# Six seams of a two-block network on one core: the last expert by columns and pieces, halves turned one by one, the last output tile in two parts

## The reference

```
for layer in (0, 1):                      # first block
    mix = windowed_gqa_sink(x) if layer == 0 else bidir_rglru_block(x)
    x = layer_norm(ALPHA * x + mix)
    aff = softmax(x @ w_router)           # 16 experts
    gates, idx = top_k(aff.T, 32)         # each expert picks 32 of the 256 tokens
    g, u = split(x[idx] @ w_gate_up)      # 16 x (1024 x 2048)
    out = (silu(g) * u) @ w_down * gates  # 16 x (1024 x 1024)
    x = layer_norm(ALPHA * x + scatter_add(out, idx))
for layer in (0, 1):                      # second block: even, then odd
    shift, scale, gate = split(silu(c) @ ada_w + ada_b)
    h = layer_norm_2(x) * (1 + scale) + shift
    y = even_mixer(h, ...) if layer == 0 else odd_mixer(h, ...)
    x = layer_norm_2(ALPHA * x + gate * y) * post_ln_g + post_ln_b
```

## Time and profile before

| what | value |
| --- | --- |
| median of 3 runs | 1498.08 us (1497.95 to 1499.9) |
| profiled execution | 1502.24 us, its span 1500.9 us |
| TensorE busy | 1139.1 us, 76% of the span |
| VectorE busy | 461.7 us, 31% |
| ScalarE busy | 326.6 us, 22% |
| granted TensorE clock, mean | 0.89 of 2.4 GHz |
| read from memory | 498.92 MB, 333 GB/s over the span |
| share of the chain of waits | DMA 50%, PE 39%, DVE 7%, ACT 3% |

### The profile page before, as it was taken

One profiled execution on the slowest core, in us unless ns is written; L12 is line 12 of the kernel. 1 busy time (PEld: TensorE's weight loads), 2 busy tenths in 40 slices (PEclk: granted clock), 3 DMA queues, 4 the chain that ended last, 5 costly groups with the idle time before them and its releaser, 6 DMA issues.

```text
span 1500.9 us, 19478 instructions
## 1 busy us (share of the span) xinstructions
PE 1139.1 (76%) x8579; PEld 651.7 (43%) x8579; DVE 461.7 (31%) x919; ACT 326.6 (22%) x627; POOL 65.5 (4%) x88
## 2 busy tenths in 40 slices
PE   8998856678585556999885655665565699989997
PEld 7756311244132111798551112111111289745896
DVE  4535202101120100587530100100000067564674
ACT  4421110001310000365110000000000046443450
POOL 3000100000000000022000000000000000000000
PEclk9999978789787979899998878888888899999999
DMA  9957999999999999929999999999999954214630
GB/s 300 358 198 280 388 425 424 427 417 422 426 422 427 425 425 424 318 59 334 412 410 425 427 424 428 427 425 426 427 427 425 410 196 148 78 50 145 214 109 29
DMA packets 89197, 501.29 MB, mean 334 GB/s; under 512 B 6950, under 2 KB 15604, under 8 KB 56344
## 3 DMA queue, kind: packets, MB, share of 16 engines
q1 hardware_dynamic: 84320, 492.78, 81.2%
q10 hardware_dynamic: 3112, 5.96, 1.1%
q0 software_dynamic: 1680, 1.30, 0.3%
HBM read 498.92 MB, written 1.10 MB: 333 GB/s over the span
## 4 chain that ended last, share of the span: by engine, by line
DMA 50%; PE 39%; DVE 7%; ACT 3%; issue 1%; POOL 1%; SPq 0%; DVEq 0%; ACTq 0%
DMA weight_spare<-in_moe_w_gate_up 16%; DMA weight_ring<-in_moe_w_gate_up 13%; DMA weight_spare<-in_moe_w_down 10%; DMA weight_ring<-in_moe_w_down 6%; PE bank L335 5%; PE bank L1340 5%; PE bank L611 3%; PE bank L336 3%; PE bank L338 3%; PE bank L337 3%; PE bank L1366 3%; DMA weight_ring<-in_even_w_in 2%; PE bank L1746 2%; PE bank L381 2%; DMA weight_spare<-in_ada_w 1%; DVE weight_ring_rounded L376 1%
## 5 line engine op out<-in xcount | busy, mean ns | idle before, releaser
L1340 PE MATMUL bank<-weight_ring,expert_tokens 128*32 128x512 f32 x1904 | 286.3, 736 | 172.8 <-DMA weight_ring<-in_moe_w_gate_up 167.8
L1340 PEld LDWEIGHTS bank<-weight_ring,expert_tokens 128*32 128x32 f32 x1904 | 61.6, 123 | 372.8 <-DMA weight_ring<-in_moe_w_gate_up 205.1
L1366 PE MATMUL bank<-weight_ring,actT 128*32 128x256 f32 x1920 | 155.1, 482 | 69.4 <-DMA weight_ring<-in_moe_w_down 60.6
L1530 DVE TENSOR_TENSOR act<-silu,bank 128x256 f32<-128x256 f32 x32 | 13.4, 420 | 414.9 <-ACT silu L1655 414.9
L1366 PEld LDWEIGHTS bank<-weight_ring,actT 128*32 128x32 f32 x1920 | 72.8, 133 | 139.6 <-issue 54.8
L1655 ACT ACTIVATE silu<-bank 128x256 f32<-128x256 f32 x32 | 12.3, 384 | 463.4 <-PE bank L1340 463.4
L1541 DVE COPY expert_outs<-bank 32x256 f32<-32x256 f32 x64 | 26.8, 418 | 255.8 <-PE bank L1366 254.7
L376 DVE TENSOR_TENSOR weight_ring_rounded<-weight_ring,weight_ring_rounded 128x1024 fp32r<-128x1024 f32 (+1 forms) x76 | 88.2, 1222 | 17.1 <-ACT weight_ring_rounded L360 16.9
L360 ACT CAST weight_ring_rounded<-weight_ring 128x1024 fp32r<-128x1024 f32 (+1 forms) x72 | 69.9, 1044 | 24.6 <-DMA weight_ring<-in_attn_w_qkv 12.0
L1669 ACT COPY expert_outs<-bank 32x256 f32<-32x256 f32 x64 | 23.3, 363 | 233.2 <-PE bank L1366 232.4
L381 PE MATMUL bank<-ident 128*128 128x128 f32 x434 | 56.0, 290 | 3.9 <-DMA ident<-in_k_ident 3.9
(11 more groups left out here) (519 smaller groups left out, 1834.4 us busy)
## 6 DMA issues: line engine op xcount, KB each, us to landing
weight_ring<-in_moe_w_gate_up SPq DMA_DIRECT2D x119, 2048.0 KB, 32.4
weight_ring<-in_moe_w_down SPq DMA_DIRECT2D x60, 2048.0 KB, 32.1
weight_spare<-in_moe_w_gate_up SPq DMA_DIRECT2D x9, 2048.0 KB, 35.6
weight_ring<-in_ada_w SPq DMA_DIRECT2D x8, 2048.0 KB, 13.2
weight_ring<-in_even_w_in SPq DMA_DIRECT2D x5, 2048.0 KB, 14.1
weight_ring<-in_odd_w_in SPq DMA_DIRECT2D x5, 2048.0 KB, 8.5
weight_spare<-in_ada_w SPq DMA_DIRECT2D x4, 2048.0 KB, 17.4
weight_ring<-in_lru_w_in SPq DMA_DIRECT2D x4, 2048.0 KB, 24.5
```

The costliest lines, as they stand in the source:

```text
L1340: last = pe.matmul(up[CAP * j:CAP * (j + 1), :], B.xs[:, t, e * CAP:(e + 1) * CAP], w[:, t % 2, :, j, :], start=(t == 0), stop=(t == T - 1))
L1366: last = pe.matmul(K[3][CAP * q:CAP * (q + 1), 0:QC], B.actT[i][:, s, j * CAP:(j + 1) * CAP], w[:, jj, s, q, :], start=(j == 0 and s == 0) ...
```

## The change

1. The `down` units of expert 15, in both layers, hold one half of the columns each (512) with all rows, and SyncE loads each in four transfers, one for each `j`. TensorE takes the pieces as they land, in products of 128 columns (`last_outs_tensor`), columns 0 into bank 3 and columns 1 into bank 1. The products with `back` for columns 0 stand after the first piece of columns 1. Copies and moments go by column halves, the moments of both halves of the tokens on VectorE in both layers.
2. `turn_x_tensor` and `modulated_tensor` turn half 0 when it is ready, with a number of identity products between the halves. The other identity products are fewer: 26 to 14 and 36 to 34 after the expert layers, 12 to 2 before the recurrent products, 12 to none and 16 to 3 around the even stage's turns, 36 to 24 and 16 to 3 around the odd stage's, 14 to 8 in layer 0's routing; between the halves stand 8, 3 and 16.
3. `x_low` is formed in four quarters: the first before the logits, the three others between the two parts of `hot`. The gather waits for each quarter where it needs it.
4. In `FIRST_UNITS` of layer 1 two `ada` units stand ahead of two expert units.
5. ScalarE rounds a pair of modulated tiles as soon as it is there.
6. In the odd stage half 1's second column half is computed, gated, added and measured in two parts of 256 columns, the last normalising step and the store go by column halves, and statistics are of 256 columns each.

```diff
-    ((2, 0), (None, 6), (3, 2), (4, SPARE), (None, 3), (5, 0), (None, 1), (None, 4), (None, 5), (0, 2), (1, SPARE),
+    ((2, 0), (None, 6), (3, 2), (4, SPARE), (None, 3), (5, 0), (None, 1), (0, 2), (1, SPARE), (None, 4), (None, 5),
...
-    def turn_x_tensor(self, stage, banks):
+    def turn_x_tensor(self, stage, banks, between=0):
 
         sig, pe, x = self.sig, self.pe, self.B.x
         for half in range(H):
+            if half:
+                self.idle_products_tensor(banks[5], between)
...
+            if name.startswith("down") and name.split("_")[1] == str(NE - 1):
+                (dst, src), = self.unit_parts(name, B.slot[slot])
+                for i in range(PACK):
+                    sp.dma_start(dst[:, i], src[:, i]).then_inc(*sig.tell(f"last{name[-1]}{i}_loaded", ("arrived", name, i), by=16))
+                continue
...
+        sp.wait_ge(*sig.after("x", "odd", 0))
+        sp.dma_start(out[:, 0, :], B.x[:, 0, :]).then_inc(*sig.tell("output_stored", ("stored",), by=16))
+        for c in range(2):
+            cols = slice(c * 512, (c + 1) * 512)
+            sp.wait_ge(*sig.after("last_tokens", c))
+            sp.dma_start(out[:, 1, cols], B.x[:, 1, cols]).then_inc(*sig.tell("output_stored", ("stored",), by=16))
...
+            if e == NE - 1:
+                rows = d["moe_w_down"][layer][e].rearrange("(j c s) n -> c j s n", j=PACK, s=2)
+                return [(slot.rearrange("p (j s n) -> p j s n", j=PACK, s=2), rows[:, :, :, k * 512:(k + 1) * 512])]
...
-            self.idle_products_tensor(K[5], 14)
+            self.idle_products_tensor(K[5], 8)
...
-        pe.wait_ge(*sig.after("x_low", stage, 1))
...
+            if e == NE - 1:
+                self.last_outs_tensor(layer)
+                next(side, None)
+                break
...
-        self.idle_products_tensor(K[5], 36 if layer else 26)
+        self.idle_products_tensor(K[5], 34 if layer else 14)
+    LAST_BANKS = (3, 1)
+    def last_outs_tensor(self, layer):
+        sig, pe, B, K = self.sig, self.pe, self.B, self.B.bank
+        stage, e, grp = f"moe{layer}", NE - 1, (NE - 1) // PACK
+        def pieces(c, js):
+            name = f"down{layer}_{e}_{c}"
+            w = self.plain(name).rearrange("p (j s q n) -> p j s q n", j=PACK, s=2, q=PACK)
+            for j in js:
+                pe.wait_ge(*sig.after("arrived", name, j))
+                for s in range(2):
+                    for q in range(PACK):
+                        last = pe.matmul(K[self.LAST_BANKS[c]][CAP * q:CAP * (q + 1), 0:P], B.actT[e % 2][:, s, j * CAP:(j + 1) * CAP],
+                                         w[:, j, s, q, :], start=(j == 0 and s == 0), stop=(j == PACK - 1 and s == 1))
+            if j == PACK - 1:
+                last.then_inc(*sig.tell("experts_down", ("last_down", stage, c), ("free", name)))
+        def back(c):
+            for q in range(2):
+                pe.wait_ge(*sig.after("last_outs", stage, c, q))
+            for half in range(H):
+                pe.matmul(K[self.SUM_BANKS[2 * half + c]], B.back[:, grp, half * P:(half + 1) * P],
+                          B.outs[grp % 2][:, c * 512:(c + 1) * 512], start=False, stop=True).then_inc(
+                    *sig.tell("experts_back", ("summed", stage, half, c)))
+        pe.wait_ge(*sig.after("back", stage, 1))
+        for before in range(1, PACK):
+            for q in range(2):
+                pe.wait_ge(*sig.after("outs", stage, e - before, q))
+        self.idle_products_tensor(K[5], 2)
+        pieces(0, range(PACK))
+        pieces(1, (0,))
+        back(0)
+        pieces(1, range(1, PACK))
+        self.idle_products_tensor(K[5], 2)
+        back(1)
+    def last_outs(self, c, q):
+        r, o = (NE - 1) % PACK, c * 512 + q * P
+        return (self.B.outs[(NE - 1) // PACK % 2][CAP * r:CAP * (r + 1), o:o + P],
+                self.B.bank[self.LAST_BANKS[c]][CAP * q:CAP * (q + 1), 0:P])
...
+                    pe.wait_ge(*sig.after("x_low", stage, half, 2 * t // T))
...
-        def low(half):
+        def low(half, part):
+            tiles = slice(part * T // 2, (part + 1) * T // 2)
             v.wait_ge(*sig.after("x_high", stage, half))
-            v.tensor_tensor(B.x_low[:, half], B.x[:, half, :].rearrange("p (c t) -> p t c", t=T), B.x_high[:, half], ALU.subtract).then_inc(
-                *sig.tell("x_low", ("x_low", stage, half)))
+            v.tensor_tensor(B.x_low[:, half, tiles], B.x[:, half, :].rearrange("p (c t) -> p t c", t=T)[:, tiles],
+                            B.x_high[:, half, tiles], ALU.subtract).then_inc(*sig.tell("x_low", ("x_low", stage, half, part)))
 
...
+        v.wait_ge(*sig.after("router_parts", stage, 0))
+        low(0, 0)
-        low(0)
...
-        low(1)
...
+            if part == 0:
+                for half, tiles in ((0, 1), (1, 0), (1, 1)):
+                    low(half, tiles)
...
+        def outs(c):
+            v.wait_ge(*sig.after("last_down", stage, c))
+            for q in (0, 2):
+                v.tensor_copy(*self.last_outs(c, q)).then_inc(*sig.tell("vector_moved", ("last_outs", stage, c, 0)))
+
+        def part(half, c):
+            v.wait_ge(*sig.after("summed", stage, half, c))
+            v.bn_stats(B.stats[:, half, 6 * c:6 * c + 6], K[self.SUM_BANKS[2 * half + c]]).then_inc(
+                *sig.tell("moments", ("moments", stage, half, c)))
+
         def moments(half):
-            for c in range(2):
-                v.wait_ge(*sig.after("summed", stage, half, c))
-                v.bn_stats(B.stats[:, half, 6 * c:6 * c + 6], K[self.SUM_BANKS[2 * half + c]]).then_inc(
-                    *sig.tell("moments", ("moments", stage, half, c)))
+            part(half, 1)
+            v.wait_ge(*sig.after("moments", stage, half, 0))
...
+        outs(0)
+        for half in range(H):
+            part(half, 0)
+        outs(1)
...
-            if half == 0 and layer == 1:
+            if half == 0:
                 moments(1)
...
-    def experts_moments_scalar(self, stage):
-
-        sig, a, B, K = self.sig, self.a, self.B, self.B.bank
...
+        for c in range(2):
+            a.wait_ge(*sig.after("last_down", stage, c))
+            for q in (1, 3):
+                a.copy(*self.last_outs(c, q)).then_inc(*sig.tell("scalar_moved", ("last_outs", stage, c, 1)))
...
-        for half in range(H):
-            pe.wait_ge(*sig.after("x", "moe0", half))
-        self.turn_x_tensor("recurrent", K)
-        self.idle_products_tensor(K[5], 12)
+        self.turn_x_tensor("recurrent", K, 8)
+        self.idle_products_tensor(K[5], 2)
...
-    def modulated_tensor(self, stage, banks):
+    def modulated_tensor(self, stage, banks, between):
...
+            if half:
+                self.idle_products_tensor(banks[5], between)
...
-        for pair in range(T // 2):
-            both = slice(2 * pair, 2 * pair + 2)
-            a.wait_ge(*sig.after("modulated", stage, pair))
-            a.copy(hi[:, both, :], lo[:, both, :]).then_inc(*sig.tell("h_rounded", ("h_rounded", stage, pair)))
+            for here in (pair - 1, pair):
+                both = slice(2 * here, 2 * here + 2)
+                a.wait_ge(*sig.after("modulated", stage, here))
+                a.copy(hi[:, both, :], lo[:, both, :]).then_inc(*sig.tell("h_rounded", ("h_rounded", stage, here)))
...
-        self.idle_products_tensor(K[5], 12)
-        self.modulated_tensor("even", K)
-        self.idle_products_tensor(K[5], 16)
+        self.modulated_tensor("even", K, 3)
+        self.idle_products_tensor(K[5], 3)
...
-        self.idle_products_tensor(K[5], 36)
-        self.modulated_tensor("odd", K)
-        self.idle_products_tensor(K[5], 16)
+        self.idle_products_tensor(K[5], 24)
+        self.modulated_tensor("odd", K, 16)
+        self.idle_products_tensor(K[5], 3)
...
+        names = "odd_out0", "odd_out1"
+        self.out_part_tensor("odd", [K[i] for i in self.ODD_OUT[0:2]], (B.y_odd_hi, B.y_odd_lo), lambda j: ("odd_y", j // 2), names,
+                             (("odd_taken", 6), ("odd_taken", 7)), 0, range(T))
+        w, rows = self.out_weights(names), slice(P, 2 * P)
+        for i, (c, at, n) in enumerate(self.ODD_LAST):
+            pe.wait_ge(*sig.after(*(("sgu_sum", 1), ("sgu_sum", 3), ("odd_y", 0))[i]))
+            for j in range(T):
+                last = self.product(K[self.ODD_OUT[2 + i]][:, 0:n], (B.y_odd_hi[:, j, rows], B.y_odd_lo[:, j, rows]),
+                                    (w[c][0][:, j, at:at + n], w[c][1][:, j, at:at + n]), start=(j == 0), stop=(j == T - 1))
...
+    ODD_LAST = ((0, 0, 512), (1, 0, 256), (1, 256, 256))
...
+    def last_tokens_vector(self):
+        sig, v, B = self.sig, self.v, self.B
+        x, moments = B.x[:, 1, :], 0
+        for i, (c, at, n) in enumerate(self.ODD_LAST):
+            cols = slice(c * 512 + at, c * 512 + at + n)
+            tmp = B.odd_tmp[c][:, at:at + n]
+            v.wait_ge(*sig.after("out_product", "odd", 1, i))
```

(20 more changed lines are left out.)

56 lines of the change are left out of this document (15 added, 41 removed).

## The result

The changed kernel takes 1487.49 us (median of 4 runs, 1486.74 to 1488.96) beside 1498.99 for the kernel before: ratio 0.9926, 95% interval 0.9914 to 0.9939. It is 11.5 us faster. The forecast was 20.2 us and 1478; the range ended at 1488. So the time lies inside the range by half a microsecond, while the gain is little more than half of the one forecast. Two terms account for most of the difference: the new order of the loads costs 6 us where 0.4 was to be won, and 2.4 us of seam b belonged to the one execution that was profiled.

What follows compares the result with a forecast made beforehand. Expert layers were taken as bound by weight transfers, mixers by TensorE, so shorter seams shift what follows. Six terms summed to 20.2 us: 1502.24 profiled became 1482.0, less 4.2 to the median gave 1478, range 1472 to 1488.

Steps and rivals of the forecast that it cites:

- b: Seam from expert layer 0 to the recurrent stage: first product sooner after the last weights, gain 9.0 us, bounds 6 and 9.5.
- a: Routing of layer 0: expert 0 starts earlier through `x_low` in quarters, gain 3.5 us, bounds 2.2 and 4.
- c: Routing of layer 1: `ada` units loaded earlier end TensorE's wait, gain 0.4 us, bounds -1 and 0.8.
- d: Seam to the even stage: earlier `x` and interleaved roundings, gain 2.8 us, bounds 1 and 4.
- e: Seam to the odd stage: identity products fill the gap, roundings come earlier; gain 3.5 us, bounds 2 and 3.9.
- f: The end of the kernel: smaller last column parts and split store, gain 1.0 us, bounds 0.5 and 1.5.
- R1: Rival: expert tails stay at 1.2 GHz, costing 3 us before the recurrent and 2 before the even stage; 1483; chance 0.17.
- R2: Rival: recurrent stage doesn't move with its start, as `lru0`'s weights come with the stream; 4 to 5 us stay, 1482.5; chance 0.09.
- The cover: Recurrent stage: slack absorbs `lru0`'s cast waiting for its weights; price 0, up to 4 us if the gates wait.
- R3: Rival: TensorE, less busy, runs three stages' first passes at 1.2 GHz; up to 36.8 us, 1515; chance 0.03.

Runs made afterwards that it cites:

- exp. 4: The kernel before, unchanged, run again for a second profile: 1499.08 us, span 1496.7.
- experiment 11: The kernel before with only the last expert by columns and pieces and its moments on VectorE: 1489.88 us, ratio 0.9933.
- experiment 6: The changed kernel with the numbers of identity products of the kernel before: 1491.68 us, ratio 0.9950 to the kernel before.
- the ninth experiment: The changed kernel turning both halves together at all three seams, identity products between them moved ahead: 1487.63 us, ratio 0.9916 to the kernel before.
- experiment 2: The changed kernel with layer 1's two `ada` units one place further back, behind one expert unit: 1481.76 us, ratio 0.9888 to the kernel before.
- experiment 1: The changed kernel with layer 1's first units in the former order, `ada` units behind both expert units: 1481.53 us, ratio 0.9888 to the kernel before.
- experiment 8: The changed kernel with `ada` units behind one expert unit and 46 identity products for 34 after expert layer 1: 1480.44 us, ratio 0.9877 to the kernel before.
- 10: The changed kernel with `x_low` formed by halves at its former places: 1490.25 us, ratio 0.9934 to the kernel before.

## Why the prediction came out as it did

Per interval in us, from the profiles. "Rows 1 to 9" and "exp. 4" are two profiles of the kernel before; "changed" is the changed kernel.

| interval | rows 1 to 9 | exp. 4 | changed | forecast gain | gain beside exp. 4 |
| --- | --- | --- | --- | --- | --- |
| start to expert 0 | 149.6 | 147.9 | 145.8 | 3.5 (a) | 2.1 |
| expert 0 to first recurrent product | 476.6 | 473.9 | 467.4 | 9.0 (b) | 6.5 |
| that to the `ada` issue | 74.0 | 73.7 | 73.7 | 0 | 0 |
| that to first even product | 525.2 | 525.6 | 527.0 | 3.2 (c, d) | -1.3 |
| that to first odd product | 175.7 | 175.7 | 172.5 | 3.5 (e) | 3.2 |
| that to the end | 99.8 | 99.9 | 99.0 | 1.0 (f) | 0.9 |

The last column sums to 11.4, beside 11.5 by the medians. That the time came inside the range is luck: c's term lies 5 us outside its bounds, and what held the sum is that R1 and R2, which the lower end of the range covers, didn't come and that d gave more than forecast.

**a: right.** Over all thirteen profiles expert 0 starts 3.1 us earlier (146.35 for 149.45), and undoing it costs 2.8. The place moves by 1 us between the profiles with the quarters and by 2.5 between those without.

**b: the mechanism was right, the size was of one execution.** The last piece lands 0.9 to 1.2 us later (456.0 us behind expert 0 for 455.1 and 454.8; forecast 0.9), and from there the first product takes 11.4 us (11.55 worked out). Beside rows 5 the gain is 9.2. But 2.4 us of that was a clock that stayed at 1.2 GHz longer in that execution. I then took 4.2 us off to come from the profiled time to the median, as if they lay elsewhere. The same 2.4 us were counted twice. Of the 6.5 that are left, single edits show the tail with 3.6 (experiment 11), the identity products with 2.1 (6) and turning half 0 early with 1.0 (9). R1 didn't come: the granted clock was 1.00 in the tail. One premise was wrong: the forecast says runs of 2 KB instead of 4 KB, but the former units read two neighbouring rows of 4 KB in one, `(s n)`, so in runs of 8 KB. The pages of the profiles agree: with the tail alone there are 4288 more packets under 8 KB, and four units in runs of 2 KB are 4096. The sum doesn't use the 4 KB.

**The recurrent stage: right, R2 out.** `lru0` lands at 632.7 and is cast 5.8 us earlier, not 13, yet the stage's output products moved by 13.1 us. The cover was there.

**c: the step that failed.** "two 2 MB loads queued behind, which empties the queue for some 0.4". 5.1 us of transfers are missing. I compared when the `ada` slots come free with when the units behind are issued, and not with what was still in flight. SyncE had issued its last unit by 703.7, the transfers ran on to about 715, and the slot came free at 718.5. One more unit of 5 us ahead of the wait closes the gap (experiment 2). With the old order the changed kernel takes 1481.5, a gain of some 17 to 18 us; the mis-sized term alone is 6.

**d: undersized.** Without the hole (experiment 1) the interval in the fourth row is 520.6, so seam d with the faster routing gains 4.6 to 5.0, where c and d together had 3.2 and upper bounds of 4.8. The tail alone brings as much here: 520.4. With TensorE ready sooner, the narrow weights, their cast and ScalarE's normalisation set the start, as the prediction had it. Three things were missed. The narrow weights didn't land 0.9 later (506.6 us behind the `ada` issue in experiment 1, for 506.4 and 507.4 in the kernel before). The identity products of before were themselves late by 1.8 us. And against that, the few identity products left let the clock fall before the turn (R3 in small: 1.3 us, experiment 8). Why the 2 KB runs cost 1 us in layer 0 and none that shows in layer 1 stays open.

**e and f: right**, 3.2 for 3.5 and 0.9 for 1.0. Of e, some 1.6 us again hang on the clock: where the clock stayed up behind the same wait, the former code took 174.1 (experiment 11) for 175.7.

The single edits add up roughly: tail 9 to 10, identity products 4 to 5, `x_low` 3, end 1, order -6. That is 11 to 13 for the 11.5 measured. It is no proof, since the edits overlap: at the even seam the tail alone brings 5.3 and the identity products alone 4.2, all together without the hole 5.0. Item 5 of the change, the earlier rounding, has no run of its own; with the former numbers of identity products the odd seam takes 174.1 with it (experiment 6) and without it (11), so there it brings nothing until they are fewer.

## What to carry to other kernels

A load that waits for its slot in a queue in order costs the wait, less the transfers that are still in flight when it begins. Before moving a load forward, subtract these from the wait; one 2 MB unit more ahead of it was worth 5.7 us here. And profile a kernel twice before taking a seam's length from it: what one execution lost to the clock is no gain of the change, and must not be taken off a second time on the way to the median.

## What the runs showed of the hardware

The same code with the same wait met different clocks. At the odd seam TensorE had worked through some 8 us of identity products and the turn of half 0 and then waited 1.9 us, in five profiles alike: in three the clock fell and the 32 records behind half 1 took 4.9 to 5.2 us, in two it stayed up and they took 3.74. At the even seam it fell in all four profiles with a wait of 2.4 to 3.3 us before the turn (experiments 1, 2, 10 and the changed kernel), and after 1.95 us in the ninth experiment it did not.
